# The last expert's down product in two column stages, each with its own scatter and squares

## The chip, the cores and the metric

The kernel runs on one core of a Trainium2 chip. The metric is the device time of one execution in microseconds (us), the median of several runs; lower is better.

## The reference, cut to what matters

A one-layer encoder over 256 frames of 1024 columns, all in f32: a mixing block, cross-attention into 256 memory tokens, then a routed expert block and a last RMSNorm. Only its end matters here:

```python
gu = xb @ w_gate_up[e] + b_gate_up[e]          # 32 experts, 4 of them for each frame
act = (x_lin + 1) * (x_glu * jax.nn.sigmoid(SWIGLU_ALPHA * x_glu))
y = act @ w_down[e] + b_down[e]
acc = acc.at[tok].add(y * g[:, None])          # scatter of the expert's rows into the sum
h = h + acc
return h * lax.rsqrt(mean(h * h) + 1e-5) * g_final
```

## The kernel before, in words

The 32 experts' weights, 12 MB each, are streamed from HBM into a ring of SBUF slots; SyncE (SP) issues every load on its DMA queue, in the order of a transfer plan, each behind a wait on how many chunks TensorE has used. An expert is six chunks of 2 MB: four for the gate and up product, two for the down product. Each expert handles at most 64 frames at a time (`CAP`). A product has 64 rows as its stationary side, so the two halves of 512 output columns go to the two column halves of the array (rows 0 to 63 and 64 to 127 of one PSUM bank). Every f32 product is two MATMUL instructions in the trace; two that go to different column halves, or read different row halves, run side by side.

Per expert, TensorE gathers the rows (L873), turns them (L898), multiplies by gate and up (`gate_up`, L927), turns gates and activations (L938, L946), adds the down bias by a bf16 product (L951), multiplies by down (`down`, L969) and scatters (`scatter_part`, L983): the 64-row result, evicted by ScalarE (ACT) to SBUF (`copy`, L1057), is multiplied by the gates into the running sum of two frame tiles (`t` or `c` = 0, 1; 128 frames by 1024 columns each), which lies in four PSUM banks for the whole block.

The order of the work at the end is written out by hand. The chunks come as: gate and up of the last expert (31), down of expert 30, down of expert 31. TensorE's queue holds: gate and up of 31; the first half of down of 30; turning of 31's activations (`turn_act_last`) and the bias of 31; the second half of down of 30; scatter of 30 into tile 0; down of 31; scatter of 30 into tile 1; scatter of 31 into both tiles. The last 2 MB chunk is loaded in four pieces of 512 KB (L517), and behind them the last norm's gain `gfin`, 4 KB read once for each of 128 partitions (L518).

ACT evicts both results, then skips the code for frames beyond 64 an expert (`more_rounds`, L406 to L415, not needed with this input), loads the activation table of Sqrt (L1062), and for each tile takes the sum of squares over 1024 columns (L1277) and its root (L1280). VectorE (DVE) multiplies tile 0 by the gain into `acc_gained` (L1685), forms 1/root with one Newton step for each tile on its own (`newton`, L1303 to L1306), and writes tile 1 in two halves from PSUM (L1695), while ACT scales tile 0 in two halves (L1285). SP stores the four 256 KB quarters (L529).

Of the kernel before, what the change touches and what calls it, by code (L numbers as in the profile page):

```python
# [19 lines left out]
F32 = mybir.dt.float32  # L20
# [19 lines left out]
E = 32  # L40
# [80 lines left out]
DOWN_USED = {e: PLACE_OF[e, PER_EXPERT - 1] + 1 for e in (E - 2, E - 1)}  # L121
HI_BUFS, LO_BUFS = 4, 4
# [29 lines left out]
def program(nc, x, mem, g_mix, w_in, w_pool, pool_scale, conv_w, w_out, g_xattn, g_mem, w_q, w_k,  # L152
            w_v, w_o, g_moe, w_router, b_router, w_gate_up, b_gate_up, w_down, b_down, g_final, out):
    with ExitStack() as ctx:
# [64 lines left out]
        h_squares = at("h_squares", 16, [P, TC, D])  # L219

# [14 lines left out]
        stat = sb("stat", [P, 5, 4, TC])  # L235
        eps = sb("eps", [P, 1])
        warm = sb("warm", [P, 1])
# [67 lines left out]
        end_root, end_out, end_rstd = sem("end_root"), [sem("end_out0"), sem("end_out1")], sem("end_rstd")  # L305

# [86 lines left out]
        acc_gained = at("acc_gained", 10, [P, D])  # L393
        assert SLOT_OF[PAIRED_FROM - 1] == 0 and 0 not in AGAIN_SLOTS
        first_gained = sem("first_gained")
        tail_in = [sem(f"tail_in{r}") for r in range(4)]
# [6 lines left out]
        def more_rounds(eng, most, body, first):  # L403
# [3 lines left out]
            with eng.If(most > CAP):  # L407
                first()
                for b in range(1, ROUNDS):
                    with eng.Fori(0, E) as e:  # L410
                        with eng.If(eng.value_load(cnt_i[0:1, bass.ds(e, 1)], min_val=0, max_val=SEQ) > CAP * b):
                            k = eng.snap(k_reg, min_val=0, max_val=SEQ * TOP_K // CAP)
                            body(b, e, k)
                            eng.reg_add(k_reg, k_reg, 1)
            return eng.snap(k_reg, min_val=0, max_val=SEQ * TOP_K // CAP)  # L415
# [3 lines left out]
        def _(sp):  # L419
# [82 lines left out]
            for n, into, used_up in TRANSFERS[BY_SLOT:-1]:  # L502
# [91 lines left out]
        def _(pe):  # L594
# [360 lines left out]
            def down(s, par, wait_chunk, last=False, between=None, by_half=False):  # L955
                pe.wait_ge(aT_ok, s + 1)
                if not last:
                    bias_down(par)
                act_rows, bank = (sig_last, bank_y_last) if last else (actT, bank_y)
                for h in range(DOWN):  # L960
                    w = halves_of(slots[SLOT_OF[TOTAL - 1]][:]) if last and h == DOWN - 1 else wait_chunk(GATE_UP + h)
                    for r in range(4):
                        if last and h == DOWN - 1:
                            pe.wait_ge(tail_in[r], 16)
                        if r % 2 == 0:
                            w_half = w[r // 2]()
                        lhsT = act_rows[:, r * P + CAP * h:r * P + CAP * (h + 1)]
                        for half in range(2):
                            mm = pe.matmul(ps[CAP * half:CAP * (half + 1), bank, :], lhsT,  # L969
# [5 lines left out]
                    if between is not None and h == 0:  # L975
                        between()

# [740 lines left out]
```

## Time and profile before

| | us |
|---|---|
| median of 3 runs | 1112.75 (1112.29 to 1113.15) |
| the profiled execution, its own time | 1112.3 |
| its span, first to last instruction | 1110.6 |
| TensorE busy in the span | 1077.2 |

The profiled execution stands 0.45 us below the median of the runs, and 1.7 us of its time lie outside the span. In the rows below, PE is TensorE's products and PEld its weight loads, SPq is SP's sequencer with its DMA issues, and "x" counts instructions. Times are from the start of the span.

### The profile page before, as it was taken

What the parts mean: (1) busy time and instruction counts of PE and PEld (TensorE: products, weight loads), DVE (VectorE), ACT (ScalarE), POOL (GpSimd) and SP (SyncE); (2) the same over time, 40 slices, a digit from 0 to 9 for tenths busy, and PEclk for the clock granted to TensorE, in tenths of its full rate; (3) what the DMA queues carried; (4) which work ended last, traced back from release to release, by engine and by line L of the source; (5) the groups of instructions that cost most, each with busy time, mean ns of one, the idle gap of its engine ahead of it and who ended that gap; (6) DMA issues with size and microseconds to landing.
All of it is one profiled execution on the core that took longest, in us unless ns stands there. A gap on an engine that the chain in (4) does not pass through costs nothing.

```text
span 1110.6 us, 12654 instructions
## 1 busy us (share of the span) xinstructions
PE 1077.2 (97%) x5407; PEld 486.9 (44%) x5408; DVE 266.8 (24%) x540; ACT 196.6 (18%) x322; POOL 27.7 (2%) x59
## 2 busy tenths in 40 slices
PE   8999999999999999999999999899999999999996
PEld 7998998433333333333333333333333333333332
DVE  7576654311111111111111111111110111111112
ACT  7534553201111111111111111111010111111102
POOL 7200000000000000000000000000000000000000
PEclk9999999999999999999999999999999999999999
DMA  9976558899999999999999999999999999999995
GB/s 346 339 255 213 204 220 343 341 393 425 429 427 427 435 431 431 429 430 434 430 430 429 430 433 433 431 431 430 429 431 431 433 431 433 427 428 427 426 430 217
DMA packets 44630, 437.93 MB, mean 394 GB/s; under 512 B 4464, under 2 KB 22304, under 8 KB 27424
## 3 DMA queue, kind: packets, MB, share of 16 engines
q1 hardware_dynamic: 44480, 437.09, 94.3%
q8 instruction: 45, 0.74, 0.3%
q14 instruction: 9, 0.07, 0.0%
q10 hardware_dynamic: 96, 0.02, 0.0%
HBM read 435.47 MB, written 1.05 MB: 393 GB/s over the span
## 4 chain that ended last, share of the span: by engine, by line
PE 73%; DMA 24%; DVE 2%; ACT 1%; issue 0%; DVEq 0%; POOL 0%; ACTq 0%; POOLq 0%
PE ps L927 27%; DMA pair<-in_w_gate_up 24%; PE ps L969 15%; PE ps L638 6%; PE ps L695 6%; PE ps L983 4%; PE ps L873 4%; PE ps L898 2%; PE ps L946 2%; PE ps L909 1%; PE ps L661 1%; PE ps L938 1%; PE ps L951 1%; PE ps L607 0%; PE ps L787 0%
## 5 line engine op out<-in xcount | busy, mean ns | idle before, releaser
L927 PE MATMUL ps<-pair,xT 128*64 128x512 f32 x1872 | 418.1, 603 | 20.6 <-DMA pair<-in_w_gate_up 20.4
L927 PEld LDWEIGHTS ps<-pair,xT 128*64 128x64 f32 x1872 | 133.3, 139 | 300.3 <-issue 267.4
L969 PE MATMUL ps<-pair,sig 128*64 128x512 f32 x880 | 193.7, 592 | 0.0
L1604 DVE TENSOR_SCALAR glu<-ps 128x512 f32<-128x512 f32 x32 | 22.1, 691 | 648.9 <-PE ps L927 648.9
L969 PEld LDWEIGHTS ps<-pair,sig 128*64 128x64 f32 x880 | 61.5, 136 | 116.2 <-issue 111.1
L1226 ACT ACTIVATE sig<-glu 128x512 f32<-128x512 f32 x31 | 19.5, 629 | 462.4 <-DVE glu L1604 462.4
L1057 ACT ACTIVATE xg_sb<-ps 128x512 f32<-128x512 f32 (+1 forms) x64 | 37.8, 590 | 290.8 <-PE ps L969 238.4
L1347 DVE TENSOR_TENSOR w_lo<-ring,w_hi 128x1024 fp32r<-128x1024 f32 x56 | 70.2, 1262 | 53.4 <-ACT w_hi L1057 52.3
L1057 ACT ACTIVATE w_hi<-ring 128x1024 fp32r<-128x1024 f32 x56 | 58.9, 1060 | 60.1 <-PE ps L638 32.1
L983 PE MATMUL ps<-xg_sb,g_sb 64*128 64x512 f32 x248 | 61.9, 616 | 0.7 <-ACT xg_sb L1057 0.7
L873 PE MATMUL ps<-h_rows,sel_rstd 128*64 128x512 f32 x248 | 60.1, 605 | 0.0
L1598 DVE TENSOR_TENSOR xT<-ps,gain_moe 128x512 f32<-128x512 f32 x31 | 21.4, 691 | 86.2 <-PE ps L898 86.2
L983 PEld LDWEIGHTS ps<-xg_sb,g_sb 64*128 64x128 f32 x248 | 21.3, 186 | 40.9 <-issue 39.3
L946 PEld LDWEIGHTS ps<-ident,glu 128*128 128x128 f32 x128 | 17.9, 209 | 26.0 <-issue 26.0
L873 PEld LDWEIGHTS ps<-h_rows,sel_rstd 128*64 128x64 f32 x248 | 15.1, 136 | 23.5 <-issue 23.5
L946 PE MATMUL ps<-ident,glu 128*128 128x128 f32 x128 | 23.9, 310 | 0.0
L898 PE MATMUL ps<-ident,xg_sb 128*128 128x128 f32 x124 | 23.2, 309 | 0.6
L638 PE MATMUL ps<-hn_hi,w_hi 128*128 128x256 f32 x160 | 23.2, 288 | 0.0
L1608 DVE SCALAR_TENSOR_TENSOR lin<-lin,glu 128x512 f32<-128x512 f32 x32 | 22.1, 692 | 1.4
L638 PE MATMUL ps<-hn_lo,w_hi 128*128 128x256 f32 x160 | 22.5, 283 | 0.0
L638 PE MATMUL ps<-hn_hi,w_lo 128*128 128x256 f32 x160 | 22.5, 283 | 0.0
L1605 DVE TENSOR_SCALAR lin<-ps 128x512 f32<-128x512 f32 x32 | 21.8, 680 | 0.0
(227 smaller groups left out, 778.6 us busy)
## 6 DMA issues: line engine op xcount, KB each, us to landing
pair<-in_w_gate_up SPq DMA_DIRECT2D x42, 4096.0 KB, 37.3
pair<-in_w_down SPq DMA_DIRECT2D x22, 4096.0 KB, 39.1
pair<-in_w_gate_up SPq DMA_DIRECT2D x33, 2048.0 KB, 18.4
pair<-in_w_down SPq DMA_DIRECT2D x12, 2048.0 KB, 17.1
half<-in_w_gate_up SPq DMA_DIRECT2D x10, 1024.0 KB, 8.5
ring<-in_w_in SPq DMA_DIRECT2D x8, 1024.0 KB, 13.3
shifted<-in_w_gate_up SPq DMA_DIRECT2D x4, 2048.0 KB, 11.4
shifted<-in_w_down SPq DMA_DIRECT2D x3, 2048.0 KB, 9.1
```

The source lines that it names most:

```text
L638: mm = pe.matmul(bank[:, (j % 2) * SEQ:(j % 2 + 1) * SEQ], w[:, k, :], src[:, k, :], start=(n == 0 and k == 0), stop=(n == 2 and k == KC - 1),
L695: mm = pe.matmul(ps[:, bank_row[r], :], src[:, k, t * P:(t + 1) * P], w[:, half * HALF:(half + 1) * HALF], start=(n == 0 and k == 0), stop ...
L873: mm = pe.matmul(ps[CAP * half:CAP * (half + 1), bank_xg, :], sel_rstd[:, t, :], h_rows[:, t, half * HALF:(half + 1) * HALF], start=(t == ...
L898: mm = pe.transpose(ps[:, bank_t[0], j * P:(j + 1) * P], xg_sb[:].rearrange("s (p a) -> s a p", a=4)[:, j, :], ident[:])
L927: mm = pe.matmul(ps[CAP * half:CAP * (half + 1), bank, :], lhsT, columns_of(cols, half), start=False, stop=(c == GATE_UP - 1 and a == 1), ...
L946: mm = pe.transpose(ps[:, bank, j * P:(j + 1) * P], act[:].rearrange("s (p r) -> s r p", r=4)[:, j, :], ident[:])
L969: mm = pe.matmul(ps[CAP * half:CAP * (half + 1), bank, :], lhsT, w_half[:, (r % 2) * D + half * HALF:(r % 2) * D + (half + 1) * HALF], sta ...
L983: mm = pe.matmul(ps[:, bank_sum[t] + half, :], gates[rws, t * P:(t + 1) * P], y[rws, :], start=False, stop=True, skip_group_check=True)
L1057: act_e.activation(dst, src, ACT.Copy).then_inc(done, 1)
L1347: dve.tensor_tensor(w_lo[j % LO_BUFS][:].rearrange("p (k n) -> p k n", **shape), src, w_hi[j % HI_BUFS][:].rearrange("p (k n) -> p k n", * ...
L1604: dve.tensor_scalar(glu[:], ps[:, 0, :], LIMIT, None, ALU.min).then_inc(glu_ok, 1)
L1608: dve.scalar_tensor_tensor(out=lin[:], in0=lin[:], scalar=1.0, in1=glu[:], op0=ALU.add, op1=ALU.mult).then_inc(step_link, 1)
```

## The change

It touches only the end, from the second half of expert 30's down on.

- **Loads.** The second down chunk of expert 30 comes in two pieces of 1 MB. The last expert's down weights are read from a copy `w_last` with another order of columns: first the columns 0 to 255 of each half of 512, for all rows (chunk `TOTAL - 2`, two pieces of 1 MB), then the columns 256 to 511 of each half (chunk `TOTAL - 1`, pieces of 1 MB, 512 KB and 512 KB). `gfin` is loaded as a single row of 4 KB, ahead of these, and spread over 128 partitions by two products of one row of ones (`spread_gain`), which DVE copies from PSUM.
- **Products.** Down of expert 31 becomes two stages of 256 columns a product (`down_last`), in two PSUM banks, each with its bias, its eviction (`y_out_last`) and its scatter (`scatter_last`). TensorE's order: second half of down of 30, `spread_gain`, the first half of the rows of stage 0, scatter of 30 into both tiles, the bias of stage 1, the rest of stage 0, scatter of stage 0, stage 1, scatter of stage 1.
- **Norm.** ACT loads the Sqrt table ahead of the eviction of expert 30. The squares of stage 0's columns, and their products with the gain, are taken after the first scatter; those of stage 1 after the second. The root takes the sum of both parts; the Newton step is done once for both tiles.
- **Outputs.** DVE scales tile 0 (two halves, from SBUF) and the stage 1 columns of tile 1 (from PSUM), ACT the stage 0 columns of tile 1. SP stores tile 0; ACT stores tile 1, on its own DMA queue, behind a wait for both writers.

The core of the diff (left out: the semaphores, the path for further rounds, and the host's making of `w_last`):

```diff
+HALVES = 2
+TAIL_ROWS = {TOTAL - 3: (0, 2, 4), TOTAL - 2: (0, 4, 8), TOTAL - 1: (0, 4, 6, 8)}
...
-        acc_gained = at("acc_gained", 10, [P, D])
+        acc_gained = at("acc_gained", 112, [P, TC, 2, HALF])
+        end_junk = at("end_junk", 120, [P, TC, 2, HALF // 2])
+        stages = [slice(f * HALF // 2, (f + 1) * HALF // 2) for f in range(HALVES)]
+        bank_stage = (bank_y_last, bank_y)
...
-            n, into, used_up = TRANSFERS[-1]
-            sp.wait_ge(chunks_used, used_up)
-            last = w_down[0, bass.ds(E - 1, 1), :, :].rearrange("o (p r) n -> p (o r) n", r=8)
-            for r in range(4):
-                sp.dma_start(slots[SLOT_OF[n]][:, D * r:D * (r + 1)], last[:, 4 + r, :]).then_inc(tail_in[r], 16)
-            sp.dma_start(gfin[:], g_final.partition_broadcast(P)).then_inc(gfin_in, 16)
+            for n, into, used_up in TRANSFERS[-len(TAIL_ROWS):]:
+                sp.wait_ge(chunks_used, used_up)
+                if n == TOTAL - 2:
+                    sp.dma_start(gfin[0:1, :], g_final.partition_broadcast(1)).then_inc(gfin_in, 16)
+                width, src = (D, expert_source(*chunk_at(n))) if n < TOTAL - 2 else (HALF, w_last[:, BIG * (n - TOTAL + 2):BIG * (n - TOTAL + 3)])
+                for r0, r1 in zip(TAIL_ROWS[n], TAIL_ROWS[n][1:]):
+                    cols = slice(width * r0, width * r1)
+                    sp.dma_start(slots[SLOT_OF[n]][:, cols], src[:, cols]).then_inc(tail_in[n, r0], 16)
 
...
-            for c in range(TC):
-                for half in range(2):
-                    part = slice(half * HALF, (half + 1) * HALF)
-                    sp.wait_ge(end_out[c], half + 1)
-                    sp.dma_start(out[0, P * c:P * (c + 1), part], out_rows[:, c, part]).then_inc(stored, 16)
+            for half in range(2):
+                cols = slice(half * HALF, (half + 1) * HALF)
+                sp.wait_ge(end_out[0], half + 1)
+                sp.dma_start(out[0, 0:P, cols], out_rows[:, 0, cols]).then_inc(stored, 16)
...
+            def bias_last(par, f):
+                for half in range(2):
+                    cols = 2 * D + half * HALF + f * HALF // 2
+                    pe.matmul(ps[CAP * half:CAP * (half + 1), bank_stage[f], 0:HALF // 2], onehot[par][:],
+                              bias[:, cols:cols + HALF // 2], start=True, stop=False, skip_group_check=True)
+
+            def spread_gain():
+                pe.wait_ge(gfin_in, 16)
+                for f, bank in enumerate((1, bank_t[0])):
+                    pe.matmul(ps[:, bank, :], ones[0:1, :], gfin[0:1, f * HALF:(f + 1) * HALF], start=True, stop=True,
+                              skip_group_check=True).then_inc(gain_spread, 1)
+
+            def down_last(f, rows_now):
+                n, wide = TOTAL - 2 + f, HALF // 2
+                for r in rows_now:
+                    if (n, r) in tail_in:
+                        pe.wait_ge(tail_in[n, r], 16)
+                    lhsT = sig_last[:, (r % 4) * P + CAP * (r // 4):(r % 4) * P + CAP * (r // 4 + 1)]
+                    for half in range(2):
+                        mm = pe.matmul(ps[CAP * half:CAP * (half + 1), bank_stage[f], 0:wide], lhsT,
+                                       slots[SLOT_OF[n]][:, HALF * r + wide * half:HALF * r + wide * (half + 1)],
+                                       start=False, stop=(r == 7), skip_group_check=True)
+                if rows_now[-1] == 7:
+                    mm.then_inc(chunks_used, 1)
+
+            def scatter_last(f, done):
+                for t in range(TC):
+                    for half in range(2):
+                        rws = slice(CAP * half, CAP * (half + 1))
+                        mm = pe.matmul(ps[:, bank_sum[t] + half, stages[f]], g_last[rws, t * P:(t + 1) * P], y_last[rws, stages[f]],
+                                       start=False, stop=True, skip_group_check=True)
...
-                bias_down((E - 1) % 2, bank_y_last)
-            down(E - 2, (E - 2) % 2, ring_chunk(E - 2), between=turn_act_last)
-            scatter_part(E - 2, 0, y_sb, g_sb)
-            down(E - 1, (E - 1) % 2, ring_chunk(E - 1), last=True)
-            scatter_part(E - 2, 1, y_sb, g_sb)
-            for t in range(TC):
-                scatter_part(E - 1, t, y_last, g_last)
+                bias_last((E - 1) % 2, 0)
+            down(E - 2, (E - 2) % 2, ring_chunk(E - 2), between=turn_act_last, tail=True)
+            pe.wait_ge(aT_ok, E)
+            spread_gain()
+            down_last(0, range(0, 4))
+            scatter(E - 2)
+            bias_last((E - 1) % 2, 1)
+            down_last(0, range(4, 8))
+            pe.wait_ge(y_early, 1)
+            scatter_last(0, early_sum)
+            down_last(1, range(8))
+            pe.wait_ge(early_gained, TC)
+            pe.wait_ge(y_ok, E)
+            scatter_last(1, sc_full)
...
+            def y_out_last(f, done):
+                act_e.wait_ge(chunks_used, TOTAL - 1 + f)
+                copy(y_last[:, stages[f]], ps[:, bank_stage[f], 0:HALF // 2], done)
+
+            def half_square(t, f, done):
+                act_e.activation(end_junk[:, t], ps[:, bank_sum[t]:bank_sum[t] + 2, stages[f]], ACT.Square, scale=D ** -0.5,
+                                 accum_out=part[:, f, t:t + 1]).then_inc(done, 1)
...
+            fetch_table(ACT.Sqrt)
             y_out(E - 2, DOWN_USED[E - 2])
-            y_out(E - 1, DOWN_USED[E - 1], last=True)
+            y_out_last(0, y_early)
+            for t in range(TC):
+                act_e.wait_ge(early_sum, t + 1)
+                half_square(t, 0, early_squares)
+                act_e.wait_ge(early_squares, t + 1)
+            y_out_last(1, y_ok)
...
-            fetch_table(ACT.Sqrt)
-            for c in range(TC):
-                act_e.wait_ge(sc_full, k * TC + (E * TC - TC + c + 1))
-                act_e.activation(h_squares[:, c, :].rearrange("p (a n) -> p a n", a=2), ps[:, bank_sum[c]:bank_sum[c] + 2, :],
-                                 ACT.Square, scale=D ** -0.5, accum_out=stat[:, 4, 0, c:c + 1]).then_inc(end_squares, 1)
-                act_e.wait_ge(end_squares, c + 1)
-                act_e.activation(stat[:, 4, 1, c:c + 1], stat[:, 4, 0, c:c + 1], ACT.Sqrt, bias=eps[:]).then_inc(end_root, 1)
...
+            for t in range(TC):
+                act_e.wait_ge(sc_full, k * TC + (E * TC - TC + t + 1))
+                half_square(t, 1, end_squares)
+            act_e.wait_ge(eps_ok, TC)
+            for t in range(TC):
+                act_e.wait_ge(end_squares, t + 1)
+                act_e.activation(stat[:, 4, 1, t:t + 1], part[:, 1, t:t + 1], ACT.Sqrt, bias=stat[:, 4, 0, t:t + 1]).then_inc(end_root, 1)
             act_e.wait_ge(end_rstd, 1)
-            act_e.wait_ge(first_gained, 1)
+            act_e.activation(out_rows[:, 1, :].rearrange("p (a n) -> p a n", a=2)[:, :, stages[0]], acc_gained[:, 1, :, stages[0]], ACT.Copy,
+                             scale=stat[:, 4, 2, 1:2]).then_inc(end_out[1], 1)
+            act_e.wait_ge(end_out[1], 2)
             for half in range(2):
-                part = slice(half * HALF, (half + 1) * HALF)
-                act_e.activation(out_rows[:, 0, part], acc_gained[:, part], ACT.Copy,
-                                 scale=stat[:, 4, 2, 0:1]).then_inc(end_out[0], 1)
+                cols = slice(half * HALF, (half + 1) * HALF)
+                act_e.dma_start(out[0, P:, cols], out_rows[:, 1, cols]).then_inc(stored, 16)
...
-            dve.wait_ge(gfin_in, 16)
+            for f, bank in enumerate((1, bank_t[0])):
+                dve.wait_ge(gain_spread, f + 1)
+                dve.tensor_copy(gfin[:, f * HALF:(f + 1) * HALF], ps[:, bank, :]).then_inc(gfin_ok, 1)
+            dve.wait_ge(gfin_ok, 2)
...
+            def half_gained(t, f, done):
+                dve.tensor_tensor(acc_gained[:, t, :, stages[f]], ps[:, bank_sum[t]:bank_sum[t] + 2, stages[f]], gain_by_half[:, :, stages[f]],
+                                  ALU.mult).then_inc(done, 1)
+
+            def add_eps(done):
+                for t in range(TC):
+                    dve.tensor_scalar(stat[:, 4, 0, t:t + 1], part[:, 0, t:t + 1], EPS, None, ALU.add).then_inc(done, 1)
+            for t in range(TC):
+                dve.wait_ge(early_squares, t + 1)
+                half_gained(t, 0, early_gained)
+            add_eps(eps_ok)
...
+            dve.wait_ge(end_squares, 1)
+            half_gained(0, 1, end_gained)
...
-            dve.wait_ge(end_squares, 1)
-            dve.tensor_tensor(acc_gained[:].rearrange("p (a n) -> p a n", a=2), ps[:, bank_sum[0]:bank_sum[0] + 2, :],
-                              gfin[:].rearrange("p (a n) -> p a n", a=2), ALU.mult).then_inc(first_gained, 1)
-            for c in range(TC):
-                dve.wait_ge(end_squares, c + 1)
-                dve.wait_ge(end_root, c + 1)
-                newton(end_linked, 5, c)
-                if c == 0:
-                    dve.sem_inc(end_rstd, 1)
+            dve.wait_ge(end_gained, 1)
+            dve.wait_ge(end_squares, TC)
+            total, (root_n, rstd, scratch) = part[:, 0, :], (stat[:, 4, i, :] for i in range(1, 4))
+            end_linked(dve.tensor_tensor(total, stat[:, 4, 0, :], part[:, 1, :], ALU.add))
+            dve.wait_ge(end_root, TC)
+            end_linked(dve.reciprocal(rstd, root_n))
+            end_linked(dve.scalar_tensor_tensor(out=scratch, in0=rstd, scalar=-0.5, in1=rstd, op0=ALU.mult, op1=ALU.mult))
+            end_linked(dve.tensor_tensor(scratch, total, scratch, ALU.mult))
+            dve.scalar_tensor_tensor(out=rstd, in0=scratch, scalar=1.5, in1=rstd, op0=ALU.add, op1=ALU.mult).then_inc(end_rstd, 1)
+            dve.wait_ge(end_rstd, 1)
             for half in range(2):
-                part = slice(half * HALF, (half + 1) * HALF)
-                dve.scalar_tensor_tensor(out=out_rows[:, 1, part], in0=ps[:, bank_sum[1] + half, :], scalar=stat[:, 4, 2, 1:2],
-                                         in1=gfin[:, part], op0=ALU.mult, op1=ALU.mult).then_inc(end_out[1], 1)
+                dve.tensor_scalar(out_rows[:, 0, half * HALF:(half + 1) * HALF], acc_gained[:, 0, half, :], stat[:, 4, 2, 0:1], None,
+                                  ALU.mult).then_inc(end_out[0], 1)
+            dve.scalar_tensor_tensor(out=out_rows[:, 1, :].rearrange("p (a n) -> p a n", a=2)[:, :, stages[1]],
+                                     in0=ps[:, bank_sum[1]:bank_sum[1] + 2, stages[1]], scalar=stat[:, 4, 2, 1:2],
+                                     in1=gain_by_half[:, :, stages[1]], op0=ALU.mult, op1=ALU.mult).then_inc(end_out[1], 1)
```

## Rows read from the trace of the kernel before

**Rows 1.** The page: the span, busy time of each engine, granted clock in 40 slices.

```profile
span 1110.6 us, 12654 instructions
...
PE 1077.2 (97%) x5407; PEld 486.9 (44%) x5408; DVE 266.8 (24%) x540; ACT 196.6 (18%) x322; POOL 27.7 (2%) x59
...
PEclk9999999999999999999999999999999999999999
```

**Rows 2.** The chain that ended last: start, length, what; from 1080 us to the end.

```profile
1092.93 7.04 PE ps L969 x32
...
1100.61 1.28 ACT L1062
...
1102.22 1.12 ACT h_squares L1277 x2
```

**Rows 3.** SP's load issues, and each one's KB and us to landing.

```profile
1048.48 0.33 SPq L421 DMA_DIRECT2D pair<-in_w_down  x1
...
pair<-in_w_down SPq DMA_DIRECT2D x1, 2048.0 KB, 38.9
...
1061.15 4.25 SPq L517 DMA_DIRECT2D pair<-in_w_down  x1
...
pair<-in_w_down SPq DMA_DIRECT2D x1, 512.0 KB, 36.1
```

**Rows 4.** Timeline of TensorE at the end: start, from first start to last end.

```profile
1087.26 0.41 PE L951 MATMUL ps<-bias,onehot 96*64 96x512 bf16 x2
1087.50 3.61 PE L969 MATMUL ps<-pair,sig 128*64 128x512 f32 x16
1091.80 1.13 PE L983 MATMUL ps<-xg_sb,g_sb 64*128 64x512 f32 x4 [0.70 <-ACT xg_sb L1057]
1092.86 7.09 PE L969 MATMUL ps<-pair,sig_last 128*64 128x512 f32 x32
...
1100.84 1.88 PE L983 MATMUL ps<-y_last,g_last 64*128 64x512 f32 x8
```

**Rows 5.** Timeline of TensorE earlier: products of other widths and tilings.

```profile
219.38 3.60 PE L995 MATMUL ps<-h_rows,ident 128*128 128x512 f32 x8
161.81 1.89 PE L808 MATMUL ps<-probsT,v_rows 128*128 128x256 f32 x8
200.00 2.01 PE L883 MATMUL ps<-h_rows,sel_rstd 128*64 128x256 f32 x8
```

**Rows 6.** Timeline of ACT, DVE and SP at the end; last, the last store's landing.

```profile
1091.15 0.60 ACT L1057 ACTIVATE xg_sb<-ps 128x512 f32<-128x512 f32 x1 [3.19 <-PE ps L969]
...
1099.99 0.60 ACT L1057 ACTIVATE y_last<-ps 128x512 f32<-128x512 f32 x1 [8.25 <-PE ps L969]
1104.69 0.29 ACT L1280 ACTIVATE stat<-stat,eps 128x1 f32<-128x1 f32 x1
1105.47 0.16 DVE L1303 RECIPROCAL stat<-stat 128x1 f32<-128x1 f32 x1 [0.23 <-DVE stat L1306]
1106.25 1.41 DVE L1695 SCALAR_TENSOR_TENSOR h_rows<-ps,stat,gfin 128x512 f32<-128x512 f32 x2
...
1107.69 0.34 SPq L529 DMA_DIRECT2D out_h<-h_rows  x1
...
out_h<-h_rows SPq DMA_DIRECT2D x1, 256.0 KB, 2.5
```

**Rows 7.** Groups by shape: busy time, mean ns of one; then instructions of one line.

```profile
L1057 ACT ACTIVATE g_sb<-ps 128x256 f32<-128x256 f32 x31 | 11.9, 383 | 27.5 <-PE ps L938 27.5
...
L1488 DVE TENSOR_SCALAR probs<-probs,smax 128x256 f32<-128x256 f32 x4 | 1.4, 354 | 0.1
...
L1315 DVE TENSOR_SCALAR n_rows<-h_rows,stat 128x1024 f32<-128x1024 f32 x1 | 0.8, 754 | 0.0
...
L407 ACTq COMPARE_BRANCH  x1: 50/50/50, 1100.1 to 1100.1; - x1
L407 PEldq COMPARE_BRANCH  x1: 3492/3492/3492, 1100.8 to 1100.8; - x1
```

More of the change, by code:

```diff
@@ L121 @@
 DOWN_USED = {e: PLACE_OF[e, PER_EXPERT - 1] + 1 for e in (E - 2, E - 1)}
+HALVES = 2
+TAIL_ROWS = {TOTAL - 3: (0, 2, 4), TOTAL - 2: (0, 4, 8), TOTAL - 1: (0, 4, 6, 8)}
+IN_PIECES = {i: sum(SLOT_OF[n] == i for n in TAIL_ROWS) for i in range(RING)}
 HI_BUFS, LO_BUFS = 4, 4
@@ L235, in program @@
         stat = sb("stat", [P, 5, 4, TC])
+        part = sb("part", [P, HALVES, TC])
         eps = sb("eps", [P, 1])
-        warm = sb("warm", [P, 1])
+        warm, warm_again = sb("warm", [P, 1]), sb("warm_again", [P, 1])
         smax = sb("smax", [P, 4, HEADS, TC])
@@ L401, in load_most, with more_rounds @@
             return eng.value_load(most_i[0:1, 0:1], min_val=0, max_val=SEQ)
-        def more_rounds(eng, most, body, first):
+        def more_rounds(eng, most, body, first, after=lambda k: None):
             k_reg = eng.alloc_register(f"rounds_{eng.engine.name}")
@@ L414, in more_rounds @@
                             eng.reg_add(k_reg, k_reg, 1)
+                after(eng.snap(k_reg, min_val=0, max_val=SEQ * TOP_K // CAP))
             return eng.snap(k_reg, min_val=0, max_val=SEQ * TOP_K // CAP)
@@ L501, in _ @@
                     sp.dma_start(shifted[n][:], expert_source(*chunk_at(n))).then_inc(shifted_full[n], 16)
-            for n, into, used_up in TRANSFERS[BY_SLOT:-1]:
+            for n, into, used_up in TRANSFERS[BY_SLOT:-len(TAIL_ROWS)]:
                 if n < WHOLE_FROM + BY_SLOT:
@@ L953, in bias_down, with down @@
                               skip_group_check=True)
-            def down(s, par, wait_chunk, last=False, between=None, by_half=False):
+            def down(s, par, wait_chunk, between=None, by_half=False, tail=False):
                 pe.wait_ge(aT_ok, s + 1)
-                if not last:
-                    bias_down(par)
-                act_rows, bank = (sig_last, bank_y_last) if last else (actT, bank_y)
+                bias_down(par)
                 for h in range(DOWN):
-                    w = halves_of(slots[SLOT_OF[TOTAL - 1]][:]) if last and h == DOWN - 1 else wait_chunk(GATE_UP + h)
+                    n = PLACE_OF[s, GATE_UP + h] if tail else None
+                    w = halves_of(slots[SLOT_OF[n]][:]) if n in TAIL_ROWS else wait_chunk(GATE_UP + h)
                     for r in range(4):
-                        if last and h == DOWN - 1:
-                            pe.wait_ge(tail_in[r], 16)
+                        if (n, r) in tail_in:
+                            pe.wait_ge(tail_in[n, r], 16)
                         if r % 2 == 0:
                             w_half = w[r // 2]()
-                        lhsT = act_rows[:, r * P + CAP * h:r * P + CAP * (h + 1)]
+                        lhsT = actT[:, r * P + CAP * h:r * P + CAP * (h + 1)]
                         for half in range(2):
-                            mm = pe.matmul(ps[CAP * half:CAP * (half + 1), bank, :], lhsT,
+                            mm = pe.matmul(ps[CAP * half:CAP * (half + 1), bank_y, :], lhsT,
                                            w_half[:, (r % 2) * D + half * HALF:(r % 2) * D + (half + 1) * HALF], start=False,
@@ L1675, in dummy @@
                 tokens_out(E, 0)
-            more_rounds(dve, most, again, dummy)
+            more_rounds(dve, most, again, dummy, once_more)
+            dve.wait_ge(end_squares, 1)
+            half_gained(0, 1, end_gained)
             ends = [0]
```

44 lines of the change are left out of this document (33 added, 11 removed).

## Prediction

> **What bounds the kernel now.** I read the page first. TensorE is busy for 97% of the span, with a granted clock of nine tenths of 2.4 GHz or more in every slice [rows 1]: its order of work, not its clock, is the thing to follow. Then the chain of waits for the last 30 us, because only they are changed. It runs on TensorE until 1100.0, with one wait, for an eviction by ACT, then over ACT's table load and squares and DVE's steps to the stores [rows 2, 4, 6]. No load stands in this part of the chain. SP's issues say how near one is: the second down chunk of expert 30 was issued at 1048.48 and landed 38.9 us later, at 1087.4, and TensorE began on it at 1087.50 [rows 3, 4]; the last piece landed at 1061.15 + 36.1 = 1097.25, when TensorE still had about 2 us of the last chunk before it [rows 3, 4]. Loads are just in time and not the bound. So the end is a sum: TensorE's queue up to the last scatter, then a serial chain over ACT, DVE and the stores.
>
> **The price of a product.** Eight f32 products of 512 columns on the whole array take 3.60 us, eight of 256 take 1.89 [rows 5]: a step of 0.43 or 0.215 us each, plus 0.16 of drain at the end. Two that run side by side in halves of the array share one step: 16 of down take 3.61 = 8 x 0.43 + 0.16, eight of scatter 1.88 = 4 x 0.43 + 0.16 [rows 4]. A change between whole array, column halves and row halves costs more: scatter's first four take 1.13 instead of 1.02, and down then starts 1.06 after them instead of 0.86 [rows 4]. I take 0.1 on leaving a tiling and 0.05 (column halves) or 0.1 (row halves) on entering one.
>
> **TensorE's new order, from 1087.26** (the first instruction that differs, expert 31's bias [rows 4]), each sum being the start of what follows:
> - bias of 256 columns: half of the 0.24 between its start and down's, so 1087.38
> - second half of down of 30: 8 x 0.43 + 0.1 = 3.54, 1090.92
> - `spread_gain`: two products of 512 columns on one row, four instructions that nothing runs beside: 4 x 0.43 + 0.1 = 1.82, 1092.74. No row has a product of one row; were two side by side it would be 0.96, which I keep as the lower end, and I take 1.82 since all rows go by columns.
> - first half of stage 0: 8 x 0.215 + 0.15 = 1.87, 1094.61
> - scatter of 30, both tiles: 4 x 0.43 + 0.2 = 1.92, 1096.53. Its eviction, 0.60, ended long before; this is the one wait removed (0.70 [rows 4]).
> - bias of stage 1 0.12 and the rest of stage 0, 8 x 0.215 + 0.05 + 0.16: 1098.58
> - wait for ACT: 256 columns take 0.383 [rows 7], with 0.05 each way 0.48: 1099.06. Nothing else is queued that could run here: stage 1 stands behind the scatter.
> - scatter of stage 0: 4 x 0.215 + 0.2, 1100.12
> - stage 1: 16 x 0.215 + 0.05 + 0.16, 1103.77
> - wait for ACT again: 1104.25. Before, scatter of 30 into tile 1 lay over the eviction [rows 4, 6]; that cover is gone.
> - scatter of stage 1: tile 0 is whole at 1104.25 + 2 x 0.215 + 0.1 + 0.16 = 1104.94, tile 1 at 1105.37.
>
> Before, tile 0 was whole at 1100.84 + 2 x 0.43 + 0.16 = 1101.86 and tile 1 at 1102.72 [rows 4]. The sums come **2.65 us later**: the spread 1.72, two waits with the drains before them 1.28, more changes of tiling some 0.47, less the wait removed 0.70 and half a bias 0.12.
>
> **What follows the sums.** Before, the table load put the first squares off to 1102.22, 0.36 after their sum [rows 2]. The load now stands behind the turning of 31, where ACT idles 3.19 before its next eviction [rows 6]: it costs nothing. The squares of 512 columns I put at 0.60, as ACT's eviction of as many [rows 6]: 1104.98 to 1106.18, 0.1 to read the sum, a root of 0.29 [rows 6]: 1106.6. DVE's product of tile 0 with the gain and the sum with stage 0's squares lie beside that. Reciprocal and three more steps take 0.78 from the first's start to the first write, as now (1105.47 to 1106.25 [rows 6]): 1107.4. Then DVE writes three pieces. Scaling from SBUF takes 0.354 for 256 columns and 0.754 for 1024 [rows 7], so some 0.49 for 512; the third is from PSUM, 0.70, half of what two take now [rows 6]: 0.49 + 0.49 + 0.70, to 1109.1. Bounds for a scaling: 0.354 to 0.754, so -0.3 or +0.5 on the end. ACT's own piece, some 0.6 as its evictions, ends by 1108.1, under this.
>
> ACT may issue only behind the last of the three, and then twice: at 1109.15 and 1109.5, if an issue costs it the 0.34 of SP's. The last store before was issued at 1107.69, landed 2.5 later, and the span ended 0.37 after that. The last issue is now 1.8 later, though the part from the sums to it is 0.85 shorter (4.13 instead of 4.97), and so is the end. For a store from ACT's queue I allow 0.4 either way.
>
> Whether the second queue gains more than issue time has a rule. The Trainium skill's page "DMA: Bandwidth & Descriptors", section "Issuing engines are not separate DMA queues", says that transfers issued by SP and ACT share the same 16 engines and that a second issuer saves only the time of issuing; no run here shows ACT's stores yet. By it the sum stands; were the queues independent the end would be at most 0.4 earlier, 1114.1.
>
> **Loads.** 512 KB less are loaded, ahead of use anyway. Second pieces come no later than the chunk did (1087.4, needed at 1089), and those of the last expert at the pace before land some 3 us ahead of need. SP's eight issues take the place of seven, up to 4.25 us each [rows 3], over 30 us ahead of use. Nothing is gained or lost. DVE's two copies of the gain, squares and products of stage 0 (two of 0.6 and two of 0.7) have 3.6 us of stage 1 over them; if they took longer, TensorE would wait before the last scatter.
>
> **Sum.** +1.8 us: 1112.3 + 1.8 = 1114.1 for the profiled execution, and against the median, which stands 0.45 above it, **1114.5**. That is 0.16%: less than 0.2%, 2.2 us, about what a measurement of this kernel can tell from no change.
>
> **Rivals.** *Slower, by the 256-column step.* The one row of 256 columns in column halves, L883, takes 2.01 for four steps, 0.46 each and not 0.215 [rows 5]. That price on the 32 steps of both stages and the 8 of their scatters would be 40 x 0.245 = 9.8 us, all on TensorE's path: 1124.3. It decides from a step of 0.23 on. Against it: L883 reads every fourth column and the new products adjacent ones, and L808 with adjacent columns goes at 0.215 [rows 5]. 4%. The Trainium skill's page "SBUF — State Buffer", section "Door 1: The DMA port swizzle", states that f32 reads pay once each falls into another 16-byte line; by that L883's price is its stride's and does not carry over, with which L808's row agrees.
>
> *Slower, by the jump.* ACT's skip of `more_rounds` took 0.05, TensorE's 3.49 [rows 7]. The change lengthens what ACT skips and puts the skip between the last eviction and the squares, where 1.1 us are covered. At TensorE's price 2.4 would show: 1116.9. Against it: ACT's own row. 8%.
>
> *Faster.* If the sums came no later, because the spread lay under the eviction of 30 and changes of tiling cost nothing, only the shorter end would be left: 1112.75 - 0.85 = 1111.9, within 0.2%. Below 1110.5 the stores would have to gain over 1 us as well. TensorE has no idle time but 0.70 to hide it in [rows 4]. 5% for below 1110.5.
>
> *The early part isn't early.* If squares of stage 0 ran only after stage 1, 1.3 us of them and 0.7 of DVE would return: 1116.5. 3%.
>
> **How the numbers follow.** The sum as worked out has 80%; its small unknowns (spread, six changes, two waits, three writes, the store) make about +-1 us, so a quarter of that, 20%, lies above 1114.95. Faster by over 0.2%: 5%; slower: 20 + 4 + 8 + 3 = 35%; within: 60%. The range runs from 1112.6 (spread at its lower end, changes of tiling free, writes at 0.354) to 1117.0 (the jump), and leaves out the strided price and the faster end.
>
> **What would show it.** Right: scatter of stage 1 begins near 1104.2, two idle gaps of about 0.5 before the scatters, spread 1.8 long, the last store issued on ACT's queue near 1109.5, no load in the last 25 us of the chain. Wrong: steps over 0.23 in `down_last`, a wait for a piece, an ACT branch over 1 us, or a last store before 1108.

## The result, and the profile after

The changed kernel took 1117.13 us (median of 5 runs, 1115.15 to 1119.53) where the kernel before took 1112.75: a ratio of 1.003, with a 95% interval from 1.0019 to 1.0042. A second set of nine runs (the first experiment) gave 1115.88 against 1113.01, 1.0025 (1.0016 to 1.0035). So it is slower by 0.25 to 0.3%, 2.8 to 3.3 us by the ratios, where 1.8 was forecast. The first median stands 4.4 us above that of the kernel before and 0.13 above the upper bound of the range, 1117.0; the second lies inside it. The profiled execution took 1115.15 with a span of 1113.4; before, the span was 1110.6 [rows 1]. The two spans differ by 2.8 to 2.9, as the second set does, so this pair of traces holds that difference. To two decimals the spans are 1113.42 and 1110.56 us in the traces; the ends below are worked out with two decimals.

The page of the changed kernel: span, busy time, granted clock in 40 slices.

```profile
span 1113.4 us, 12758 instructions
...
PE 1079.6 (97%) x5453; PEld 490.7 (44%) x5454; DVE 268.6 (24%) x544; ACT 196.6 (18%) x326; POOL 27.9 (3%) x59
...
PEclk9999999999999999999999999999999999999999
```

As in [rows 1], TensorE is busy for 97% and its granted clock is nine tenths of 2.4 GHz or more in every slice, 0.99 on average in both. The clock has no part in the difference. The timeline of the changed kernel's end follows (start, from first start to last end, what; idle time before it in brackets):

```profile
1086.95 0.30 PE L990 MATMUL ps<-bias,onehot 96*64 96x256 bf16 x2
1087.08 3.60 PE L978 MATMUL ps<-pair,sig 128*64 128x512 f32 x16
1090.62 1.98 PE L996 MATMUL ps<-gfin,ones 1*128 1x512 f32 x4
1092.52 1.95 PE L1006 MATMUL ps<-pair,sig_last 128*64 128x256 f32 x16
1094.40 1.99 PE L1025 MATMUL ps<-xg_sb,g_sb 64*128 64x512 f32 x8
...
1096.45 1.90 PE L1006 MATMUL ps<-pair,sig_last 128*64 128x256 f32 x16
1098.40 0.38 ACT L1106 ACTIVATE y_last<-ps 128x256 f32<-128x256 f32 x1 [7.00 <-PE ps L1006]
1098.84 1.13 PE L1016 MATMUL ps<-y_last,g_last 64*128 64x256 f32 x8 [0.49 <-ACT y_last L1106]
1099.58 0.60 ACT L1294 ACTIVATE end_junk<-ps 128x512 f32<-128x512 f32 x1 [0.80 <-PE ps L1016]
1099.90 3.67 PE L1006 MATMUL ps<-pair,sig_last 128*64 128x256 f32 x32
1104.21 1.13 PE L1016 MATMUL ps<-y_last,g_last 64*128 64x256 f32 x8 [0.64 <-ACT y_last L1106]
1104.95 0.60 ACT L1294 ACTIVATE end_junk<-ps 128x512 f32<-128x512 f32 x1 [0.88 <-PE ps L1016]
...
1106.68 0.17 DVE L1786 RECIPROCAL stat<-stat 128x2 f32<-128x2 f32 x1
...
1107.47 0.88 DVE L1792 TENSOR_SCALAR h_rows<-acc_gained,stat 128x512 f32<-128x512 f32 x2
1107.98 0.83 SPq L539 DMA_DIRECT2D out_h<-h_rows  x2
1108.26 0.74 DVE L1794 SCALAR_TENSOR_TENSOR h_rows<-ps,stat,gfin 128x512 f32<-128x512 f32 x1
1109.04 1.04 ACTq L1355 DMA_DIRECT2D out_h<-h_rows  x2
```

Read it against [rows 4] from the first instruction that differs, the bias, to the last scatter. Before: 1087.26 to 1100.84, 13.58. Now: 1086.95 to 1104.21, 17.26. TensorE's queue is 3.68 longer: the spread stands in it with 1.90 to its successor (1090.62 to 1092.52), and two waits for ACT, 0.49 and 0.64, have taken the place of one of 0.70. A further 1.06 is the scatter of stage 0 (1098.84 to 1099.90), half of what lay behind this mark before; the rest is drains and changes of tiling. From the start of the last scatter to the end of the span it took 9.7 before (1110.56 - 1100.84) and takes 9.2 now (1113.42 - 1104.21). That gain of 0.5 should have been larger: the last issue stands 5.24 after the scatter (1109.45, the second of ACT's two: 1109.04 + 1.04 less its own 0.63) where it stood 6.85 after it (1107.69 [rows 6]), so 1.6 were gained up to there and 1.1 given back behind. What is behind is the store. Its line, ACT's two stores of the changed kernel, with the time from issue to landing:

```profile
L1355 ACTq DMA_DIRECT2D out_h<-h_rows x2: 379/505/631, 1109.0 to 1109.5; - x2
...
DMA to landing us min/median/max: 2.9/3.2/3.6
```

The last store of before landed after 2.5 [rows 6]; this one after up to 3.6. The DMA view of both kernels shows what was in the way (bytes moved in 40 equal slices of the window, then packets, MB and share by queue). Changed kernel, 1107.9 to 1113.4:

```profile
GB/s 0 0 0 0 0 119 89 283 402 357 357 373 313 372 402 372 373 387 328 417 417 373 373 402 402 372 253 60 15 30 30 30 15 30 0 0 0 0 0 0
...
q8 instruction: 1, 0.02, 1.4%
```

Kernel before, 1104.5 to 1106.5, and its four stores in the timeline:

```profile
GB/s 0 0 0 0 0 0 0 0 0 328 0 0 0 0 0 0 0 0 0 0 0 0 0 0 0 0 0 0 0 0 0 0 0 0 0 0 0 0 0 0
...
q8 instruction: 1, 0.02, 3.6%
...
1106.08 1.95 SPq L529 DMA_DIRECT2D out_h<-h_rows  x4
```

A single packet of instructions, 16 KB, moves in each window; its share, 1.4% of 16 engines over 5.5 us, is 1.2 us of one engine. Before, it went at about 1105.0, when no store had been issued: SP issued the first at 1106.08. Now it goes at about 1108.65, as the stores begin. The full rate falls off in the 27th and 28th slice, and six slices of 0.14 us at 15 to 30 GB/s follow: what is outstanding there is a tail of a few packets. That this is the packet's doing is a reading up to here; the experiments test it. The packet follows the start of TensorE's jump over the code for further rounds by 4.2 to 4.4 us in both kernels. An earlier packet of the same size goes 1.0 to 1.3 us after that start, ahead of every store (in the changed kernel at 1105.6, in the kernel before at 1101.8, by the DMA views of 1102 to 1109.5 and 1099 to 1105.5). The jump itself (the compare and branch of each engine, ns, first and last start):

```profile
L415 ACTq COMPARE_BRANCH  x1: 50/50/50, 1103.8 to 1103.8; - x1
L415 PEldq COMPARE_BRANCH  x1: 3614/3614/3614, 1104.3 to 1104.3; - x1
```

ACT's jump took 0.05, as before; TensorE's 3.6, as before, but 3.5 us later [rows 7].

### The profile page after: what moved, and what is told of

Same layout as the page of the kernel before. It is cut to its first block, busy times and chain, and to the rows that moved or that the text cites. A ratio compares the mean times of both kernels' runs of the same rounds, so it can differ in the third digit from the quotient of the medians.

```text
span 1113.4 us, 12758 instructions
## 1 busy us (share of the span) xinstructions
PE 1079.6 (97%) x5453; PEld 490.7 (44%) x5454; DVE 268.6 (24%) x544; ACT 196.6 (18%) x326; POOL 27.9 (3%) x59
## 4 chain that ended last, share of the span: by engine, by line
PE 70%; DMA 27%; DVE 2%; ACT 0%; issue 0%; POOL 0%; DVEq 0%; POOLq 0%; ACTq 0%
DMA pair<-in_w_gate_up 27%; PE ps L937 25%; PE ps L978 14%; PE ps L648 6%; PE ps L705 6%; PE ps L1025 4%; PE ps L883 4%; PE ps L908 2%; PE ps L956 1%; PE ps L919 1%; PE ps L671 1%; PE ps L948 1%; PE ps L1006 1%; PE ps L617 0%; PE ps L797 0%; PE ps L961 0%
```

## The experiments

Two theories stood ahead of the first four runs (the repeat, both on stores, and the gain by load). **Queue:** a store issued by ACT lands later than one of SP's. **Phase:** the runs spread because of something long before the end. The third came out of their traces, ahead of the other four. **Packet** (collision, in the expectations): the late landing is the instruction packet's, which now falls among the stores. Starts of the last scatter and ends of the span are given for each, so that a shift of the whole execution drops out.

**The changed kernel again**, no edit.

> The changed kernel unchanged, to see its spread again. Queue theory: ACT's stores land late (3.6 us in the profile of after, 2.5 before) and by how much differs from run to run in steps of some 2 us. Phase theory: the steps arise long before the end, from how loads, TensorE's waits for them and the clock's dips behind those waits fall. Both: spans from 1113.4 up, steps of about 2 us, median near 1117. Should the profiled execution be one of the slower, the queue theory wants the last scatter at 1104.2 as before and a later landing; the phase theory wants expert 31's bias later than 1087.0 and the same 9.2 us from the last scatter to the end.

Measured: 1115.88 (1115.06 to 1117.16), ratio 1.0025 (1.0016 to 1.0035); span 1113.3, the last scatter at 1104.22. The 9.1 of the end and the whole difference come back in another execution. Both theories had wanted a median near 1117; this one is lower, and its profiled execution was a fast one, so it doesn't tell them apart.

**All four stores on SP.**

```diff
                 sp.dma_start(out[0, 0:P, cols], out_rows[:, 0, cols]).then_inc(stored, 16)
+            sp.wait_ge(end_out[1], 2)
+            for half in range(2):
+                cols = slice(half * HALF, (half + 1) * HALF)
+                sp.dma_start(out[0, P:, cols], out_rows[:, 1, cols]).then_inc(stored, 16)
...
-            act_e.wait_ge(end_out[1], 2)
-            for half in range(2):
-                cols = slice(half * HALF, (half + 1) * HALF)
-                act_e.dma_start(out[0, P:, cols], out_rows[:, 1, cols]).then_inc(stored, 16)
```

> One part undone: all four stores on SP's queue, tile 1's behind the same wait for both writers. Queue theory: the last two land 2.5 us after issue, the span of the fastest execution falls by 1.1 to 1112.3, and the runs lie within 1 us: median about 1114. Phase theory: 1112.3 for the fastest if the queue costs its 1.1 in the profile, but the spread of 2 to 4 us stays: median about 1116. The rule on shared engines by itself (a queue costs or saves issue time only) wants no change but 0.1.

Measured: 1115.99 (1115.33 to 1118.56), 1.0026 (1.0017 to 1.0036). The last scatter is at 1107.00 and the span ends at 1116.1: 9.1 again, with no store of ACT's. The last two stores did land after 2.3 to 2.5, as the queue theory wanted, but nothing was gained by it, so ACT's queue isn't what the end is late by. The profiled execution was one of the slower, and as the phase theory wanted its bias was late (1089.74) and its end as long as before. The DMA view of 1110.7 to 1116.1 and SP's issues (ns; L543 issues tile 1's stores) show the packet, and an unexpected cost:

```profile
GB/s 0 0 0 0 121 0 91 288 379 364 349 319 46 15 15 0 30 30 319 349 394 394 394 334 394 425 349 394 395 349 425 364 394 167 0 0 0 0 0 0
...
q8 instruction: 1, 0.02, 1.2%
```

```profile
L539 SPq DMA_DIRECT2D out_h<-h_rows x2: 353/919/1485, 1110.8 to 1111.2; - x2
...
L543 SPq DMA_DIRECT2D out_h<-h_rows x2: 432/442/452, 1112.7 to 1113.2; - x2
...
DMA to landing us min/median/max: 2.3/2.4/2.5
```

The packet goes in the fifth slice, the rate falls to 15 to 30 GB/s in the middle of the stores, and SP's second issue, begun at 1111.2, takes 1.485 where the other three take 0.35 to 0.45. Here the loss is paid in the middle instead of at the end, and is as large. That the packet is what held up this issue is a reading: no run takes the packet out of this version.

**Kernel before, tile 1's two stores issued by ACT.**

```diff
-            for c in range(TC):
-                for half in range(2):
-                    part = slice(half * HALF, (half + 1) * HALF)
-                    sp.wait_ge(end_out[c], half + 1)
-                    sp.dma_start(out[0, P * c:P * (c + 1), part], out_rows[:, c, part]).then_inc(stored, 16)
+            for half in range(2):
+                part = slice(half * HALF, (half + 1) * HALF)
+                sp.wait_ge(end_out[0], half + 1)
+                sp.dma_start(out[0, 0:P, part], out_rows[:, 0, part]).then_inc(stored, 16)
...
+            for half in range(2):
+                part = slice(half * HALF, (half + 1) * HALF)
+                act_e.wait_ge(end_out[1], half + 1)
+                act_e.dma_start(out[0, P:, part], out_rows[:, 1, part]).then_inc(stored, 16)
```

> The kernel before with this part alone: tile 1's two stores issued by ACT, each behind its own half. Queue theory: slower than before by 1 us at the fastest, 1113.8, and runs spread by 2 to 4 us where the kernel before has 0.9. Phase theory: within 0.5 us of before with no more spread. Rule on shared engines: same as before.

Measured: 1112.68 (1112.19 to 1114.06), 0.9997 (0.9988 to 1.0006); last scatter 1100.85, span 1110.6, so 9.7 for the end, as without the edit. The queue theory had wanted 1113.8 at the fastest. ACT's two stores and their landing:

```profile
L1289 ACTq DMA_DIRECT2D out_h<-h_rows x2: 357/368/380, 1107.0 to 1107.7; - x2
...
DMA to landing us min/median/max: 2.5/2.5/2.5
```

With no packet among the stores, ACT's land in the 2.5 of SP's last. The second queue costs nothing and saves nothing.

**Changed kernel without TensorE's code for further rounds.** The stores, their queues and all that runs here stay; the jump has nothing to jump over.

```diff
                 turn_tokens(E)
-            more_rounds(pe, most, again, dummy)
```

> The changed kernel without TensorE's code for further rounds (left out: the jump over it and the code itself, which this input never runs), so that TensorE fetches no code behind its last scatter. Collision theory: the instruction packet of 16 KB that ran on one DMA engine at 1108.7, for 1.2 us in the middle of the stores, is gone; the last store lands 2.5 to 2.8 us after issue instead of 3.6, and from the start of the last scatter to the end it is 8.3 us instead of 9.2: fastest span 1112.5. Queue theory (ACT's stores are slow in themselves): 9.2 as before, since ACT still stores. Rate theory (four stores in 1.5 us are bound by writing): 9.2 as before.

Measured: 1114.48 (1114.06 to 1117.78), 1.0019 (1.0008 to 1.003) against 1112.8 of the same chip. TensorE's queue is unchanged (bias 1087.22, last scatter 1104.48, 17.26), and the span ends at 1112.75: 8.3 where it was 9.2. The DMA view from 1108.2 to 1112.7 has no instruction row, and ACT's stores:

```profile
GB/s 0 0 0 0 0 0 0 0 346 346 364 437 346 382 437 346 328 437 382 364 346 419 364 400 400 364 383 401 364 382 419 364 201 0 0 0 0 0 0 0
```

```profile
L1354 ACTq DMA_DIRECT2D out_h<-h_rows x2: 378/418/458, 1109.3 to 1109.7; - x2
...
DMA to landing us min/median/max: 2.4/2.5/2.6
```

The rate now stays full to its last slice, the low tail is gone, and the last store lands after 2.6 instead of 3.6. The queue theory and the rate theory (four stores in 1.5 us are bound by writing) had both wanted 9.2. The runs' times alone would not tell: the interval overlaps that of the changed kernel, 1.0016 to 1.0035, while the fastest run is 1.0 us faster (1114.06 against 1115.06).

**Kernel before without that code**, the control: the same line taken out of the kernel before.

```diff
                 turn_tokens(E)
-            more_rounds(pe, most, again, dummy)
```

> Control: the same left out of the kernel before. There the packet ran at 1105.0 to 1106.2 and the first store's data only from 1106.9. Collision theory: no change, 9.72 us from the start of expert 31's scatter to the end, span 1110.6. If code fetching costs TensorE or the end something in another way (a later barrier, say), it gets faster here too.

Measured: 1112.8 (1112.1 to 1114.22), 0.9998 (0.9989 to 1.0007); last scatter 1101.41, span 1111.1, 9.7. Nothing is gained where the packet met no store. The two together show it: the gain of 0.9 in the end isn't that of a shorter program but of the packet's place.

**Changed kernel, the gain loaded onto all partitions as before**, so without the spread.

```diff
-                if n == TOTAL - 2:
-                    sp.dma_start(gfin[0:1, :], g_final.partition_broadcast(1)).then_inc(gfin_in, 16)
...
+            sp.dma_start(gfin[:], g_final.partition_broadcast(P)).then_inc(gfin_in, 16)
...
-            spread_gain()
...
-            for f, bank in enumerate((1, bank_t[0])):
-                dve.wait_ge(gain_spread, f + 1)
-                dve.tensor_copy(gfin[:, f * HALF:(f + 1) * HALF], ps[:, bank, :]).then_inc(gfin_ok, 1)
-            dve.wait_ge(gfin_ok, 2)
+            dve.wait_ge(gfin_in, 16)
```

> One part undone: the gain is loaded for 128 partitions behind the last weights, no product spreads it and DVE copies nothing. By the sum TensorE saves the 1.91 us of the spread: the last scatter starts at 1102.3 instead of 1104.2 and the fastest span is 1111.5. If the spread lay over a wait of its own (eviction of expert 30, a piece) less comes back: the eviction ends 0.8 after the spread began and the piece has landed, so 1.9 it should be. The queue theory wants the spread of the runs unchanged, since ACT still stores.

Measured: 1114.48 (1113.09 to 1120.41), 1.0014 (1.0003 to 1.0025). TensorE's queue in its timeline:

```profile
1089.96 0.30 PE L989 MATMUL ps<-bias,onehot 96*64 96x256 bf16 x2
...
1093.53 1.89 PE L999 MATMUL ps<-pair,sig_last 128*64 128x256 f32 x16
...
1105.16 1.14 PE L1009 MATMUL ps<-y_last,g_last 64*128 64x256 f32 x8 [0.64 <-ACT y_last L1098]
```

From the bias to the last scatter it is 15.20 instead of 17.26: the spread cost 2.06, and the load that it saves was worth nothing. This profiled execution began late (below), so its span, 1114.3, is not to be set beside 1113.4; the end is 9.1, with the packet among the stores. Without the spread, the queue is 1.62 longer than before (15.20 against 13.58): the two stages by themselves cost TensorE what the shorter serial part gains, 1.6.

**Kernel before, ACT's table load moved ahead**, to behind the turning of 31, and its jump with it.

```diff
             act_out(E - 1, last=True, bank=bank_t[0])
+            fetch_table(ACT.Sqrt)
             y_out(E - 2, DOWN_USED[E - 2])
...
-            k = more_rounds(act_e, most, again, lambda: tokens_out(E))
+            k = more_rounds(act_e, most, again, lambda: tokens_out(E), lambda k: act_e.activation(warm_again[:], ones[:, 0:1], ACT.Sqrt))
...
-            fetch_table(ACT.Sqrt)
```

> The kernel before with one part alone: the Sqrt table is loaded ahead of the eviction of expert 30. By the sum the squares begin right behind their sum of 1101.86, at 1101.9 instead of 1102.22, and everything after moves by 0.3: span 1110.25, median 0.3 below before. If the first squares wait for the second tile or for the jump instead, nothing.

Measured: 1112.57 (1111.59 to 1113.82), 0.9996 (0.9987 to 1.0005). In the timeline the squares begin 1.07 after the last scatter (1.38 before [rows 2, 4]):

```profile
1102.27 1.88 PE L984 MATMUL ps<-y_last,g_last 64*128 64x512 f32 x8
...
1103.34 1.02 ACT L1278 ACTIVATE h_squares<-ps 128x1024 f32<-128x1024 f32 x1 [1.32 <-PE ps L984]
```

The end takes 9.4 (span 1111.7, in an execution that began 1.1 late) instead of 9.7. The part of the change that earns something without TensorE earns 0.3, too little for these runs to tell.

**The gain by load, and another order:** all of stage 0, scatter of 30, scatter of stage 0, bias, stage 1 (against the version with the gain loaded).

```diff
-            down_last(0, range(0, 4))
+            down_last(0, range(8))
             scatter(E - 2)
-            bias_last((E - 1) % 2, 1)
-            down_last(0, range(4, 8))
             pe.wait_ge(y_early, 1)
             scatter_last(0, early_sum)
+            bias_last((E - 1) % 2, 1)
             down_last(1, range(8))
```

> A version of the change: gain by load as in the third edit, and TensorE's order turned so that the eviction of stage 0 lies under expert 30's scatter: all of stage 0, scatter of 30, scatter of stage 0, then the bias and products of stage 1. Against the gain by load alone this takes away a wait of 0.45 and some 0.3 of changes of tiling: the last scatter starts 0.75 earlier, near 1101.5 from a bias at 1087.0, span 1110.7 if the stores still meet the packet. If the wait only moves to expert 30's eviction or to the early products, less comes back.

Measured: 1113.77 (1112.64 to 1116.7), 1.0014 (1.0005 to 1.0023); span 1110.9. TensorE's timeline:

```profile
1087.21 0.30 PE L989 MATMUL ps<-bias,onehot 96*64 96x256 bf16 x2
...
1092.88 1.95 PE L999 MATMUL ps<-pair,sig_last 128*64 128x256 f32 x16 [0.20 <-DMA pair<-in_w_last]
...
1096.58 1.03 PE L1009 MATMUL ps<-y_last,g_last 64*128 64x256 f32 x8
...
1101.93 1.14 PE L1009 MATMUL ps<-y_last,g_last 64*128 64x256 f32 x8 [0.64 <-ACT y_last L1097]
```

The first wait for ACT is gone (the scatter of stage 0 at 1096.58 shows no idle time), and the queue takes 14.72, 0.48 less than 15.20; 0.20 of what is missing is a new wait for a piece of the weights. Even so it is 1.14 over the 13.58 of before, which the shorter end (8.9, with the packet among the stores) doesn't pay back. SP's second issue took 1.416 here, begun at 1106.1 with the packet at 1106.2, though ACT issued two of the four stores: the long issue of the version with all stores on SP isn't a matter of one queue. This profiled execution came within 0.3 us of the span of before; its runs are slower by 0.14%. No version tried beat the kernel before by more than the runs can tell. This one without the code for further rounds was not run; if that took off the same 0.9, from the bias to the end it would be 22.8 where the kernel before has 23.3, an estimate from the rows above, and 0.05% is less than these runs can tell.

## Why the prediction was right, and where it was wrong

**TensorE's order: right, term by term.** Counted from the bias, the forecast put the spread at 3.66, stage 0 at 5.48, scatter of 30 at 7.35, scatter of stage 0 at 11.80, stage 1 at 12.86 and the last scatter at 16.99. The trace has 3.67, 5.57, 7.45, 11.89, 12.95 and 17.26. The spread was put at 1.82 and stands for 1.90 (2.06 by the experiment that takes it out); products of one row are priced by columns, so the lower end, 0.96, was rightly left to the range. The second wait for ACT is 0.64, not 0.48. One sum of the range doesn't come out: by the terms named for its lower end (0.86 for the spread, 0.47 for the changes of tiling, 0.3 for the writes) it is 1112.9, not 1112.6; nothing hangs on it.

**The 256-column rival is out:** 32 steps in pairs take 3.67, and (3.67 - 0.16) / 16 is 0.22, the price of adjacent columns [rows 5], not of every fourth. **ACT's jump** took 0.05, so that rival is out too, and **the early part was early**: the first squares ran at 1099.58, over stage 1.

**The serial part: right up to the last issue.** From the last scatter the forecast had squares after 0.73, the first write after 3.15, the last written after 4.85, ACT's issues after 4.9 and 5.25. The trace has 0.74, 3.26, 4.79 (1108.26 + 0.74), 4.83 and 5.24.

**The step that failed is the landing:** "The last issue before was issued at 1107.69, landed 2.5 later" was carried over, with "For a store from ACT's queue I allow 0.4 either way". I put the doubt on the queue, and the queue was innocent: ACT's stores land in 2.5 with nothing among them. By the Trainium skill's page "DMA: Bandwidth & Descriptors", section "Issuing engines are not separate DMA queues", a second issuer gives no second path; the trace agrees, 9.7 us with and without ACT issuing two of the four in the kernel before. What I missed is who else used the 16 engines. I had TensorE's jump in [rows 7] and followed it only as a price that ACT might pay. That 16 KB of code move some 4.2 us after the jump's start was to be seen in the DMA view of before. The change moves the packet later with the last scatter, by 3.7, but the first store only by 1.9 (1106.08 to 1107.98), and so brings the two together. It measured 0.9 from the last scatter to the end (9.2 against 8.3) and 1.0 in the last landing (3.6 against 2.6). The Trainium skill's page "Runtime: NRT & Kernel Launch", section "Instruction fetch mechanics", states that each engine's code comes in blocks of 16 KiB over a DMA queue of its own, and that a jump out of the fetched window waits for its block. The 16 KB packets on an instruction queue (q8) agree with it, and so do the 3.6 us of TensorE's jump, with the earlier packet 1.3 us after its start; the packet that met the stores came 0.7 after the jump's end. It calls the crossing of a block mostly hidden; here it is hidden from TensorE's own work but not from the stores.

So the forecast for the span, 1110.6 + 1.8 = 1112.4, missed 1113.4 by 1.0, of which that term is 0.9. The spread's and the second wait's small excess (0.27) was made up by a bias that came 0.31 earlier, which nothing in the forecast foresaw (1086.96 in the repeat, 1087.22 in the version without TensorE's code), so that this agreement is luck. Since +1.8 us stood close under the bound of 0.2%, one term of 0.9 carried the result over it: the likeliest case, no change that can be measured, is not what came, and "slower", with 35%, is. The median of the first set, 1117.13, missed the forecast of 1114.5 by 2.6: 0.9 of it is the packet's, and the 2 us by which it lies over its own profiled execution were not traced.

**Loads: right for the changed kernel, too sure for the one before.** "Loads are just in time and not the bound" held in the one execution read. In three relatives of the kernel before the chunk came late: from the bias to the last scatter they took 14.02, 14.01 and 13.91 instead of 13.58, and their chains name the load; that of the one with ACT's stores:

```profile
1046.57 40.85 DMA pair<-in_w_down
```

In the changed kernel, where that chunk comes in pieces, four executions took 17.26 each, or 15.20 without the spread. So the pieces may hide up to 0.4 us that the kernel before sometimes pays; no run has the pieces alone.

## What to carry to other kernels

When a change moves an engine's last work, move its jumps and what they fetch along with it in the forecast: an instruction packet shares the DMA engines with the data, and at the end of a kernel, where stores are the chain, one packet of 16 KB cost 0.9 us. Splitting the last step to start its reduction early pays, by these runs, only if the engine that bounds the kernel isn't made to wait or to do extra products for it: here 3.7 us, 2.1 of them for the spread, went into TensorE's queue for 1.6 us of a shorter serial part. And when a forecast stands just under the line that separates "no change" from "slower", its small terms decide; list every user of the resource that ends the chain before giving one of them a doubt of 0.4.

## What the runs showed of the hardware that was not expected

A packet of instructions among the stores delays them: the last landing was 3.6 with it and 2.6 without. In the two versions where the packet came within 0.1 us of SP's second issue, that issue took 1.485 and 1.416 us instead of about 0.4.

Executions differ from the first microseconds on. The same four products near the start took 1.20 in the changed kernel's profile and 2.07 in that of the version with all stores on SP (the timelines of the two):

```profile
7.97 1.20 PE L705 MATMUL ps<-w_hi,mn_hi 128*128 128x512 f32 x4 [1.42 <-DVE mn_lo L1403]
```

```profile
7.97 2.07 PE L709 MATMUL ps<-w_hi,mn_hi 128*128 128x512 f32 x4 [1.23 <-DVE mn_lo L1403]
```

The lag stayed to the end: the bias of expert 31 ran at 1089.74 there and at 1086.95 here, 2.79 apart, though the edit lies behind it. The version with the gain loaded has the same lag (2.08 for these products, the bias at 1089.96).

The granted clock reads 1.00 for both executions from 5 to 10 us, but for the second that is no reading: the first record of the granted clock in its trace stands at 13.99 us (14.14 with the gain loaded, 6.22 in the changed kernel), and the view counts time without a record as full. One execution has a record there, that of the kernel before with the early table: its granted clock of 8 to 10 us is 0.53, the lower level of 1.2 GHz for most of the stretch, and four products that ran in it took 1.91:

```profile
8.90 1.91 PE L696 MATMUL ps<-w_hi,mn_lo 128*128 128x512 f32 x4
```

The same four took 1.91 in both late executions and 1.07 in the changed kernel. So the late ones most likely ran at 1.2 GHz up to about 14 us. That is a reading by these times, since no record of the clock covers the stretch. Ahead of these products TensorE had been idle in every one of these executions (1.23 us in the late ones, 1.42 in the changed kernel, 1.65 with the early table), so what decides between them stays open. The lag explains why a span from a single profile can be off by 2.8 us, and why the ends were measured from the last scatter; whether the spread of the other runs comes from it was not traced.
